# GpSimd adds some of the expert rows: a third sum beside TensorE's and VectorE's in a two-layer hybrid decoder

## What is computed

```python
h = rms(x);  z = h @ w_in
x = x + mixed_branches(z) @ w_out          # differential attention, MLA, short convolution, gates
h = rms(x, g_ffn)                          # PEER, below, on this h
s = per head and half, (h @ w_query) . sub_keys        # 8 heads, 2 x 128 keys
top_s, top_i = top_k(s, 16)
best_s, best_c = top_k(all 256 sums of the two halves, 16)
expert = i1 * 128 + i2                     # 8 heads x 16 = 128 experts for each token
w = softmax(best_s) * gelu(u_tab[expert] . h)
x = x + sum over the 128 experts of w * v_tab[expert]
x = x + sigmoid(rms(x) @ w_ple_gate) * (p @ w_ple_proj)
```

## Time and profile before

| | |
|---|---|
| median of 3 runs | 3559.59 us (3552.55 to 3559.77) |
| the profiled execution | 3564.28 us, span 3562.5 us |
| granted TensorE clock, mean | 0.901 |
| TensorE busy | 2838.8 us (80%) |
| VectorE busy | 2520.5 us (71%) |
| ScalarE busy | 1267.3 us (36%) |
| GpSimd busy | 1337.5 us (38%) |
| moved by DMA | 1296.91 MB, of it 1073.81 MB by the gathers |

### The profile page before, as it was taken

The page is one execution under the profiler, slowest core; times in us unless marked ns, Lnnn a source line. Parts: engine busy times, 40 slices in busy tenths (PEclk is TensorE's granted clock), DMA queues, the critical chain, the costliest instruction groups (busy, mean ns, idle before and its releaser), DMA issues. The chain is left out here.

```text
span 3562.5 us, 27990 instructions
## 1 busy us (share of the span) xinstructions
PE 2838.8 (80%) x8016; PEld 1454.8 (41%) x8016; DVE 2520.5 (71%) x5181; ACT 1267.3 (36%) x3352; POOL 1337.5 (38%) x1033
## 2 busy tenths in 40 slices
PE   8899888778989778777998778878999775556556
PEld 4554635435436334433446334535446432112112
DVE  1411667787767978787768978887767986777775
ACT  2320225456123334456213334457213332223222
POOL 0000033445333443445433433345433444554552
PEclk9989898889999989988999989989999998778778
DMA  4224299899999999999999999999999999999996
GB/s 160 105 83 165 101 362 388 356 415 421 421 421 394 403 406 394 384 403 419 421 415 389 389 391 382 357 407 421 421 421 390 385 402 421 422 421 397 422 421 264
DMA packets 182970, 1296.91 MB, mean 364 GB/s; under 512 B 20384, under 2 KB 21920, under 8 KB 28192
## 3 DMA queue, kind: packets, MB, share of 16 engines
q0 software_dynamic: 147456, 1073.81, 73.5%
q1 hardware_dynamic: 35360, 221.31, 15.7%
HBM read 1292.94 MB, written 2.10 MB: 364 GB/s over the span
## 5 line engine op out<-in xcount | busy, mean ns | idle before, releaser
L596 POOL DMA_INDIRECT ring<-in_uv,experts x1024 | 1335.0, 1304 | 2178.4 <-DVE x L1354 893.8
L1478 PE MATMUL ps_sum<-ring,diag 128*128 128x512 f32 x1992 | 1160.6, 724 | 580.9 <-ACT diag L888 580.0
L1345 DVE SCALAR_TENSOR_TENSOR ring<-ring,h_ffn 128x1024 f32<-128x1024 f32 x1024 | 1236.7, 1221 | 280.6 <-DMA ring<-in_uv,experts 273.2
L1478 PEld LDWEIGHTS ps_sum<-ring,diag 128*128 128x128 f32 x1992 | 413.0, 222 | 1201.9 <-ACT diag L888 835.4
L1354 DVE SCALAR_TENSOR_TENSOR x<-ring,weight,x 128x1024 f32<-128x1024 f32 x526 | 674.9, 1283 | 129.1 <-ACT weight L892 129.0
L886 ACT ACTIVATE diag<-ident,dots 128x128 f32<-128x128 f32 x498 | 199.0, 400 | 757.3 <-DVE ring L1345 737.1
L890 ACT ACTIVATE dots<-dots 128x1 f32<-128x1 f32 x526 | 105.2, 200 | 704.2 <-DVE ring L1345 703.1
L1622 PE MATMUL ps_act<-area_h,wt 128*128 128x256 f32 x1536 | 347.0, 384 | 2.6 <-ACT area_h L612 2.6
L1750 PE MATMUL ps_act<-wt,area_h 128*128 128x512 f32 x768 | 338.5, 595 | 11.2 <-DMA wt<-in_weights 11.2
L1622 PEld LDWEIGHTS ps_act<-area_h,wt 128*128 128x128 f32 x1536 | 293.6, 192 | 62.1 <-issue 19.3
L1540 PE MATMUL ps_act<-wt,area_h 128*128 128x512 f32 (+1 forms) x704 | 303.7, 590 | 4.8 <-ACT area_h L612 4.5
(11 more groups left out here) (196 smaller groups left out, 2158.5 us busy)
## 6 DMA issues: line engine op xcount, KB each, us to landing
wt<-in_weights SPq DMA_DIRECT2D x182, 1024.0 KB
ring<-in_uv,experts POOLq DMA_INDIRECT x1024
wt<-in_weights SPq DMA_DIRECT2D x8, 832.0 KB
wt<-in_weights SPq DMA_DIRECT2D x11, 512.0 KB
wt<-in_weights SPq DMA_DIRECT2D x4, 768.0 KB
x<-in_x SPq DMA_DIRECT2D x4, 512.0 KB, 5.1
area_y<-in_keys SPq DMA_DIRECT2D x4, 512.0 KB
area_f<-in_keys SPq DMA_DIRECT2D x4, 512.0 KB
```

What stands on the lines that cost most here:

```text
L596: pool.indirect_dma_start(ring[:, row.slot, :], None, a[f"uv{row.step // 2}"][:, :], bass.IndirectOffsetOnAxis(ap=experts[:, row.step % 2, ...
L1345: dve.scalar_tensor_tensor(u, u, 1.0, h_ffn[:, row.tile, :], ALU.mult, ALU.mult, accum_out=dots[:, row.j:row.j + 1]).then_inc(dots_ready, 1)
L1478: ins = pe.matmul(ps_sum[:, b, :], diag[:, row.pe_before % DIAGS, :], ring[:, row.slot, D + b * 512:D + (b + 1) * 512], start=row.pe_first ...
```

## The change

A third sum is kept by GpSimd. pool_rows() goes through the rows due to TensorE and takes every third, unless it lies among the last 16 of its 128. For such a row ScalarE makes the column, as for VectorE, and signals pool_weight_ready. GpSimd does the addition itself, in its own queue, at the place where it would otherwise wait for the row's slot: ahead of the gather that reuses the slot. The first pool row of a tile is a product straight into pool_sum; each other is a product in place in the ring slot, a wait for it, and an addition into pool_sum. VectorE's add_sum adds pool_sum to x first and ps_sum after it; the next tile's first pool row waits for that.

pool_sum takes 1024 values a partition. Room is made: mask goes, and MLA's scores use dist scaled by -1/2^60, while MLA's queries are scaled by 2^60 (so that the distances vanish beside the scores and -1e30 still rules a key out); pT moves into area_kv, scratch into area_e; the factors are written over the dots, and weight goes.

```diff
-BY_PE = shares()
+DUE = shares()
+def pool_rows():
+    seen, out = 0, []
+    for number, by_pe in enumerate(DUE):
+        seen += by_pe
+        out.append(bool(by_pe and seen % 3 == 0 and number % ROWS < ROWS - 2 * RING))
+    return out
+BY_POOL = pool_rows()
+BY_PE = [by_pe and not by_pool for by_pe, by_pool in zip(DUE, BY_POOL)]
...
-        mask = sb("mask", [P, 512])
-        pT = sb("pT", [P, 2, HALF])
-        weight = sb("weight", [P, ROWS])
+        pool_sum = sb("pool_sum", [P, D])
-        scratch = sb("scratch", [P, 512])
+        pT = area_kv[:, 2048:2560].rearrange("p (k t) -> p k t", k=2)
+        scratch = area_e[:, 1024:1536]
...
-            pool.memset(mask[:, :], 0.0).then_inc(consts_made, 1)
-            for m in (dist, mask):
-                pool.affine_select(out=m[:, :], in_=m[:, :], ...)
+            pool.affine_select(out=dist[:, :], in_=dist[:, :], ...)
...
                     former = Row(number - RING)
-                    if former.by_pe:
+                    if former.by_pool:
+                        v, w = ring[:, former.slot, D:2 * D], dots[:, former.j:former.j + 1]
+                        pool.wait_ge(pool_weight_ready, former.pool_before + 1)
+                        if former.pool_before == POOL_BEFORE[former.number - former.j]:
+                            if former.tiles_before:
+                                pool.wait_ge(pool_sum_added, former.tiles_before)
+                            pool.tensor_scalar(pool_sum[:, :], v, w, None, ALU.mult).then_inc(pool_rows_done, 1)
+                        else:
+                            pool.tensor_scalar(v, v, w, None, ALU.mult).then_inc(pool_scaled, 1)
+                            pool.wait_ge(pool_scaled, former.pool_before + 1 - (former.tiles_before + 1))
+                            pool.tensor_tensor(pool_sum[:, :], pool_sum[:, :], v, ALU.add).then_inc(pool_rows_done, 1)
+                        pool.wait_ge(pool_rows_done, former.pool_before + 1)
+                    elif former.by_pe:
...
-                        act.activation(weight[:, j], dots[:, j], ACT.Copy, scale=gate[:, row.step % 2, row.tile, j])\
-                            .then_inc(weight_ready, 1)
+                        act.activation(dots[:, j], dots[:, j], ACT.Copy, scale=gate[:, row.step % 2, row.tile, j])\
+                            .then_inc(pool_weight_ready if row.by_pool else weight_ready, 1)
...
-                take(dve.tensor_tensor_reduce(mla_prob[b][:, 0:w], bank(w), window(mask, d, t), -1.0, HIGHEST,
+                take(dve.tensor_tensor_reduce(mla_prob[b][:, 0:w], bank(w), window(dist, d, t), -1.0 / MLA_UP, HIGHEST,
...
                 xs = x[:, 2 * (row.step % 2) + row.tile, :]
+                dve.wait_ge(pool_rows_done, POOL_BEFORE[row.number + 1])
+                dve.wait_ge(dve_rows, row.number + 1 - PE_BEFORE[row.number + 1] - POOL_BEFORE[row.number + 1])
+                dve.tensor_tensor(xs, pool_sum[:, :], xs, ALU.add).then_inc(pool_sum_added, 1)
                 dve.wait_ge(pe_rows, PE_BEFORE[row.number + 1])
-                dve.wait_ge(dve_rows, row.number + 1 - PE_BEFORE[row.number + 1])
+                dve.wait_ge(pool_sum_added, row.tiles_before + 1)
                 dve.tensor_tensor(xs, ps_sum[:, :, :].rearrange("p b n -> p (b n)"), xs, ALU.add).then_inc(sum_added, 1)
...
-                    if not row.by_pe:
+                    if not row.by_pe and not row.by_pool:
                         waiting.append(row)
```

More of the change, by code:

```diff
@@ L24 @@
 HIGHEST = 3e38
+MLA_UP = 2.0 ** 60
 DH, DHD = 4, 64
@@ L314, in shares @@
     return by_pe
-BY_PE = shares()
+DUE = shares()
[7 more added lines that the diff above has]
+BY_PE = [by_pe and not by_pool for by_pe, by_pool in zip(DUE, BY_POOL)]
 PE_BEFORE = [sum(BY_PE[:i]) for i in range(len(BY_PE) + 1)]
+POOL_BEFORE = [sum(BY_POOL[:i]) for i in range(len(BY_POOL) + 1)]
 class Row:
@@ L330, in __init__ @@
         self.pe_before = PE_BEFORE[number]
-        self.dve_before = number - self.pe_before
+        self.by_pool = BY_POOL[number]
+        self.pool_before = POOL_BEFORE[number]
+        self.dve_before = number - self.pe_before - self.pool_before
         self.tiles_before = number // ROWS
@@ L495, in trunk @@
         pe_rows = sem("pe_rows")
+        pool_rows_done = sem("pool_rows_done")
+        pool_scaled = sem("pool_scaled")
+        pool_weight_ready = sem("pool_weight_ready")
+        pool_sum_added = sem("pool_sum_added")
         sum_added = sem("sum_added")
@@ L578, in _ @@
                       allow_small_or_imprecise_dtypes=True).then_inc(consts_made, 1)
-            pool.memset(mask[:, :], 0.0).then_inc(consts_made, 1)
             pool.iota(iota[:, :], [[1, TOPK]], base=0, channel_multiplier=0,
                       allow_small_or_imprecise_dtypes=True).then_inc(consts_made, 1)
-            pool.wait_ge(consts_made, 3)
-            for m in (dist, mask):
-                pool.affine_select(out=m[:, :], in_=m[:, :], compare_op=ALU.is_ge, fill=MASKED, base=384,
-                                   pattern=[[-1, 512]], channel_multiplier=1).then_inc(consts_made, 1)
+            pool.wait_ge(consts_made, 2)
+            pool.affine_select(out=dist[:, :], in_=dist[:, :], compare_op=ALU.is_ge, fill=MASKED, base=384,
+                               pattern=[[-1, 512]], channel_multiplier=1).then_inc(consts_made, 1)
             for number in range(STEPS * STEP_ROWS):
@@ L1127, in mla_sums @@
                 op(dve.tensor_reduce(ss[:, 16:32], sk, AX, ALU.add))
-                kr2 = scratch[:, 0:64].rearrange("p (t d) -> p t d", t=2)
+                kr2 = area_e[:, 1536:1600].rearrange("p (t d) -> p t d", t=2)
                 op(dve.tensor_tensor(kr2, kr, kr, ALU.mult))
@@ L1152, in mla_rope @@
                 link()
-                krs = scratch[:, 64:128].rearrange("p (t d) -> p t d", t=2)
+                krs = area_e[:, 1600:1664].rearrange("p (t d) -> p t d", t=2)
                 cos, sin = rope_cos[:, g0:g0 + 2, :], rope_sin[:, g0:g0 + 2, :]
@@ L1353, in add_row @@
                     dve.wait_ge(dve_rows, row.dve_before)
-                dve.scalar_tensor_tensor(xs, ring[:, row.slot, D:2 * D], weight[:, row.j:row.j + 1], xs, ALU.mult, ALU.add)\
+                dve.scalar_tensor_tensor(xs, ring[:, row.slot, D:2 * D], dots[:, row.j:row.j + 1], xs, ALU.mult, ALU.add)\
                     .then_inc(dve_rows, 1)
@@ L1397, in make_tables @@
                 dve.wait_ge(tables_loaded, 16 * N_TABLES)
-                dve.wait_ge(consts_made, 5)
-                products = scratch[:, 0:4 * DHD].rearrange("p (l c d) -> p l c d", l=DEPTH, c=2)
+                dve.wait_ge(consts_made, 3)
+                products = ring[:, 2, 0:4 * DHD].rearrange("p (l c d) -> p l c d", l=DEPTH, c=2)
                 pairs = lam_in.rearrange("p l (c two) d -> p l c two d", two=2)
@@ L1406, in make_tables @@
                         make(dve.tensor_scalar(dq_gain[:, layer, h:h + 1], col("g_dq", layer), float(DHD) ** -0.5 / SLOPES[h], None, ALU.mult))
-                    make(dve.tensor_scalar(mq_gain[:, layer:layer + 1], col("g_mq", layer), float(MQK) ** -0.5, None, ALU.mult))
+                    make(dve.tensor_scalar(mq_gain[:, layer:layer + 1], col("g_mq", layer), float(MQK) ** -0.5 * MLA_UP, None, ALU.mult))
                     make(dve.tensor_scalar(dsub_gain[:, layer:layer + 1], col("g_dsub", layer), 1.0 - LAMBDA_INIT[layer],
                                            None, ALU.mult))
-                dve.memset(scratch[:, 0:1], 0.0).then_inc(consts_made, 1)
-                dve.wait_ge(consts_made, 7)
+                dve.memset(ring[:, 2, 0:1], 0.0).then_inc(consts_made, 1)
+                dve.wait_ge(consts_made, 5)
                 for layer in range(DEPTH):
```

2 lines of the change are left out of this document (1 added, 1 removed).

## The result

| | before | after |
|---|---|---|
| median | 3559.55 us | 3716.4 us (3713.62 to 3717.29, 4 runs) |
| ratio | | 1.0436, 95% interval 1.0418 to 1.0454 |
| span of the profiled execution | 3562.5 us | 3711.8 us |

The change makes the kernel slower by 157 us, 4.4%. The prediction had 3594 us, in a range of 3515 to 3660: the side was right, the size was not.

The account below looks back on a forecast made before the run. DMA at 421 GB/s bounds most of the span, VectorE rank/top-k, VectorE and TensorE chains attention. 36 - 8 + 0 + 6 = +34 us on 3564.3 gave 3598, as median 3594 us; own range 3570 to 3640, 8 in 10 3515 to 3660.

Parts of the forecast that it names:

- What bounds the kernel: DMA leads in most of the span, VectorE in rank/top-k, VectorE and TensorE chains in attention; DMA lacks some 92 us.
- steps 2 and 3: TensorE's relief in rank/top-k, -8 us; in attention, at most -32 won against at most +45 lost, taken as 0 us.
- What a pool row costs VectorE: VectorE cannot run a dot or row addition while GpSimd's pair runs: 0 to 3.1 us lost per pool row, mean 1.55.
- Where that is paid: Rank/top-k: 23 pool rows at 1.55 us, +36 us (0 to 71); attention: 23 at 1.95 us, +45 us at most.
- step 4: The 92 pool rows where DMA leads: VectorE has 53 of 200 us free, so cover holds, 0 us.
- What a pool row costs GpSimd: Product about 1.05 us and addition 1.05 to 2.05 us on GpSimd: 3.1 us for the pair, 2.1 at the least.
- step 5: Ring turn: gathers wait behind the pair; a pool slot needs 18.7 of 19.9 us, fits narrowly, 0 us.
- rival C: GpSimd is late with gathers once a pool row holds its queue over 6.7 us: 3686 us; chance 0.15 together with B.
- A: VectorE is not held; TensorE's relief is all there is: -34 us, about 3525 us; chance 0.28.
- B: The whole pair is lost wherever VectorE leads or shares the lead: +118 us, 3678 us; chance 0.15 together with rival C.
- D: Relief and lock weigh the same and cancel, DMA's bytes unchanged: within 7 us of 3560; chance 0.10.
- The small edits: Mask folded into dist, pT, scratch and weights in place, memset and one select fewer on GpSimd: no time.

Follow-up runs that it names:

- left_out: The changed kernel, but the 138 pool rows are added by nobody: GpSimd writes one column instead of product and addition; 3532.04 us, ratio 0.9912.
- tax_only: As left_out, but VectorE does two more instructions per pool row, some 1.65 us, and GpSimd waits for both before freeing the slot; 3620.58 us.
- hold_full: The changed kernel, but GpSimd writes zeros for 5.7 us per pool row instead of product and addition, pool rows left out of the sum; 3624.1 us.

## Why the prediction was wrong

*What bounds the kernel*: right in the main. Relief bought 31 us, within the 92 that DMA lacked. The terms of steps 2 and 3 for it, -8 and two thirds of -32, make -29; the split is less good, since by rows, from the kernel before to left_out, the rank stages give 15 us and the two kinds of attention 15. That TensorE's clock falls when its work is taken away has no term in the sum.

*What a pool row costs VectorE*: the mechanism was there, and the extremes show it: the dot's maximum went from 1277 (rows 6) to 3415 ns. That the size fits, 1.55 us predicted and 1.63 measured over dots and row additions, is luck: 1.55 was half of a pair of 3.1 us, 1.63 is 28% of one of 5.73. In the rank stages, for which the 1.55 was meant, it is 1.0. The Trainium skill, SBUF — State Buffer, section "Who interferes with whom", calls the shared ports an exclusive lock and says, of VectorE's two-port modes, that it lasts for the whole instruction. The addition's rows agree with that. The product's don't: a product of 2.86 us let a row addition through that started 2.1 us after it. The measurement decides.

*Where that is paid*: wrong in part. The sum charged 23 pool rows in rank at 1.55 and 23 in attention at half of 1.95, 36 + 22 = 58 us; tax_only shows 89. Two things failed. The rows were counted in windows that are shorter than the stages: the rank stages have 28 pool rows and lost 44 us (1.6 each), differential attention has 22 and lost 29. And the 0 of step 4 for the rows where DMA leads did not hold in MLA: DMA at 417 to 421 GB/s and VectorE 76 to 79% busy, and still 32 pool rows lost 19 us. For the other rows of that kind the 0 held (-3 us, and +5 in step 3). Why MLA gives no cover, while step 3 does, is not shown; that VectorE's work stands there in the chains to TensorE and ScalarE is an argument.

*What a pool row costs GpSimd*: wrong, and the larger error. The pair was priced at 3.1 us from a select and an iota; it is 5.73. The addition's 2.34 us at the least is near my 2.05 (and the estimate of 2.25 us from the Trainium skill, GPSIMD Engine Reference, section 3.1); the product, 2.84 us at the least, is not a pass at the select's price. What misled was to take one price for every one-input operation of an engine.

*The ring's turn* (step 5, rival C): the mechanism was named and its term set to 0, "it fits, narrowly", with 1.2 us to spare. Put 5.73 for 3.1 into its own sum and the turn is 21.3 of 19.9 us; the run with 5.7 us held costs 92 us. With the 3.1 us as priced, the table of held times has the cost between 6 and 44 us. So the zero was too low even then: the cost starts between 2.2 and 4.6 us held, well ahead of the 6.7 us that the sum gave as the point. The largest part of hold_full's loss, 39 us, is in MLA, where a row came every 2.5 us, and 18 us in the first 24 rows, where every third is a pool row: a turn there has less to spare than in step 3, from which its parts were taken. This 0 is the step of the sum that cost most.

*Rivals*: A (no standing) fell by the dot's maximum. B priced the lock at 116 us, measured 89. C's was 3686 us with 1 us beyond the point. In the measured kernel lock and queue come together and add up, where I took them as alternatives with 0.15 between them. D fell.

*The small edits*: right, 0 us.

## What to carry to other kernels

An engine that issues the gathers is not free for arithmetic to the extent that it is idle: here 2.2 us of extra work at every third to sixth row cost nearly nothing and 5.7 us cost 92 us, although the engine was 38% busy before. Price an operation by a row of that very operation on that engine; where there is none, and the answer hangs on it, work out the ring's turn at the upper bound too. Count what a stage holds over the whole stage, not over a window in it. And before moving work between engines for which SBUF room has to be made, ask what the same room brings as one more buffer: here it was worth 25 us, nearly the whole 31 us that free relief would have brought.

## What was not expected of the hardware

- GpSimd's tensor_scalar with a column as scalar takes 2.84 us at the least for 128x1024, its copy 1.04 us, its zeros 0.94 us, its two-input addition 2.34 us, and a two-input product whose second input is a broadcast column 1.89 us.
- tensor_scalar, the longest of these, makes VectorE stand less than the addition does: 0.49 us a product in the mean and 1.28 us an addition, by what the dots and row additions that overlap either lie over 1.22 and 1.28 us.
- Some VectorE instructions with one input stood as well: of eight tensor_scalar instructions of 128x32 on stats, 0.18 us each in left_out, two took 2.31 us in the changed kernel.
- Rows 5 are no single case. In the kernel before, the 635 gathers that start under a dot or row addition take 1.68 us in the median and mostly end 0.81 us after it; the 168 that meet no two-input instruction of VectorE take 0.94.
- The gathers' median is 1144 ns in the kernel before and 1112 in the changed kernel, but 946 in hold_full, where zeros stand in the pair's place.
